# Both scan directions in one hop, full-width products behind the state hops, and a third one-hot that two engines share

## The chip, the cores and the metric

The program runs on one core of a Trainium2 chip. The metric is the device time in microseconds of one execution; lower is better. Engines by their names in the profile: PE is TensorE (its matrix products), PEld its weight loads, DVE VectorE, ACT ScalarE, POOL GpSimd, SP SyncE, which issues the transfers.

## The reference, cut to what matters

Two layers of a hybrid backbone over 640 tokens (512 latent, 128 context). In every layer one projection feeds three token mixers, and an expert stage follows. The change touches two places of a layer.

First, the RWKV-7 scan, for 4 heads of 64 and both directions d, with differential attention beside it (8 heads, softmax of two score maps):

```python
def step(S, inp):
    r_t, w_t, k_t, v_t, kk_t, a_t = inp
    sa = einsum('bhij,bhj->bhi', S, -kk_t)
    S = S * w_t[:, :, None, :] + sa[..., None] * (kk_t * a_t)[:, :, None, :] + v_t[..., None] * k_t[:, :, None, :]
    return S, einsum('bhij,bhj->bhi', S, r_t)
# run forwards for d = 0 and backwards for d = 1; the two outputs are added
```

Second, the gates of the expert layer. Per token, 128 chosen experts (a row number, a column number and a weight each) are written out as a dense 128 x 128 table of weights: the sum over the choices of (row one-hot x weight) times (column one-hot).

## The kernel before, in words

Stages run one after another, each a block in which every engine has its own instruction stream and the streams meet at semaphores. The order of work on an engine is the order of the code.

**Mixing** (`mix_stage`, once per layer). The scan works in chunks of 64 tokens, two to a tile of 128, with 5 tiles. For every step (5) and every direction (2) come 14 *hops* in a row, listed in `HOPS`. One hop is one *slot*: PE makes the hop's products in PSUM, then DVE (and in some hops ACT) copies or adds them into SBUF, and PE waits for those copies (`byv`, `bya`) before the next hop. The hops are:

- `pairs` and `lower`: products of keys with keys and receptances within a chunk (64x64 blocks), masked by DVE into `mb`, `mk`, `pwt` and `x`; `lower` also turns the keys (`bt`).
- `square1` to `square5`, `inverse`: a triangular inverse by repeated squaring. Each makes `pwt` products (L1171), `pw` products (L1175) and `x` products (L1182); DVE copies `pwt`, ACT copies `pw`, DVE adds to `x`. `inverse` also multiplies the masked keys with the values (L1188), which ACT copies into `tv`.
- `rhs`, `sa`, `state`, twice (one per chunk): the state hops, a strict chain through the state `sz`. In `state` PE makes the state's products with the receptances (L1207), the state's update (L1210, L1211) and the outputs within the chunk (L1219); DVE updates `szt` and `sz` (L1377, L1381), and in `state1` adds the outputs to `outT` (L1390).

Four heads times two chunks make 8 products of 64x64 in a group; heads and chunks lie on different halves of the partitions. A float32 product shows as two records in the trace.

Attention runs beside it in pieces. A *unit* is one head and one tile (40 units: 32 over 768 keys, the last 8 over 128). Three slots hold the pieces of a unit: behind a slot's hop, PE makes scores (L1236 to L1240) and, every second unit, value products (L1272), or turns probabilities (L1253); DVE takes row maxima (L1398), reciprocals and combines (L1412); ACT does the exponentials (L1303), scales (L1308) and copies (L1315). So the pieces are spread over about 129 of the 140 slots.

**Gates** (`gates_stage`, once per layer). Tokens come 16 at a time (an *octet*, 24 of them, two to a turn). DVE makes five tables of 128x2048 bf16: `ea` and `ob` (comparisons), and three weighted copies `oa` (L2135), since the weight is split into three bf16 parts. PE makes 48 products of them (L2152), then 4 products of the expert layer's hidden values (L1580, 128x384 float32), ACT copies the result (L2178) and, once a turn, applies the gelu (L1591). SP writes the results to DRAM and loads weights.

## Time and profile before

| what | value |
|---|---|
| median of 3 runs | 4585.85 us (4578.81 to 4588.88) |
| the profiled execution, its own time | 4598.13 us |
| its span, first to last instruction | 4596.3 us |
| mean granted clock of TensorE | 0.926 |
| mixing, first layer | 352.9 to 714.4 us |
| mixing, second layer | 2608.0 to 2973.9 us |
| gates, first and second layer | 1293.9 to 1436.7 us, 3553.4 to 3695.9 us |

The two mixing stages are 727 us of the span and the two gates stages 285 us. A stage's time is read from its own stretch; the shares over the whole span mix stages with different limits. A granted clock of 1.00 is the upper of PE's two levels (2.4 GHz), 0.50 the lower (1.2 GHz).

### The profile page before, as it was taken

The page shows a single profiled execution, that of the slowest core. Times are in us where ns is not written, and L with a number is a line of the kernel's source. Part 1 is how long each engine was busy: PE and PEld are TensorE (multiplying, and loading weights), DVE is VectorE, ACT ScalarE, POOL GpSimd, SP SyncE. Part 2 cuts the span into 40 slices and gives each one's busy share as a digit, 9 for nine tenths or more (in the row PEclk, how much of TensorE's full clock was granted, in tenths as well). Part 3 has the DMA queues.
Part 4 walks back from the last instruction along what each step waited for, and adds up shares of the span by engine and source line. Part 5 has one row for each costly group of instructions (what it writes and reads, how often), then busy time and mean ns, then how long its engine had stood idle before and what let it go on. Part 6 is the DMA issues. An engine that isn't in the chain of part 4 may idle for free. (4 is left out here: it accounts for less than half of the span.)

```text
span 4596.3 us, 73822 instructions
## 1 busy us (share of the span) xinstructions
PE 4136.2 (90%) x28014; PEld 3374.0 (73%) x28014; DVE 3534.4 (77%) x6601; ACT 1516.6 (33%) x2264; POOL 1390.6 (30%) x1046
## 2 busy tenths in 40 slices
PE   7988987899978999999989799879997989999997
PEld 5966776875556888888879477669654778888885
DVE  3456654589998999999855566437799989999996
ACT  4424532421123333333252445233111333333333
POOL 0000000006513666666400000000255055666662
PEclk8988977999989999999999789689998999999998
DMA  6230002229978999999721300031599899999994
GB/s 236 69 115 5 2 2 93 92 58 408 411 245 300 409 408 407 405 408 400 300 93 42 118 2 2 34 115 47 185 412 354 247 357 408 409 404 403 405 405 184
DMA packets 408301, 1079.58 MB, mean 235 GB/s; under 512 B 37728, under 2 KB 183392, under 8 KB 401376
## 3 DMA queue, kind: packets, MB, share of 16 engines
q1 hardware_dynamic: 260576, 539.10, 32.2%
q0 software_dynamic: 147456, 536.94, 29.4%
q8 instruction: 163, 2.67, 0.2%
q14 instruction: 106, 0.87, 0.1%
HBM read 996.47 MB, written 79.43 MB: 234 GB/s over the span
## 5 line engine op out<-in xcount | busy, mean ns | idle before, releaser
L1623 POOL DMA_INDIRECT ring<-peer_u_rows,rows x512 | 657.6, 1284 | 2221.5 <-DVEq L2020 1540.1
L1623 POOL DMA_INDIRECT ring<-peer_v,rows x512 | 708.4, 1384 | 416.1 <-DVE acc L2436 341.5
L1580 PE MATMUL ps<-h,u 128*128 128x384 f32 x2048 | 683.7, 493 | 20.8 <-PEq L1652 17.3
L204 PE MATMUL ps<-vhi,wlo 128*128 128x512 f32 x1536 | 608.4, 396 | 73.5 <-DVE wlo L2415 71.9
L2436 DVE SCALAR_TENSOR_TENSOR acc<-ring,act,acc 128x1024 f32<-128x1024 f32 x508 | 645.4, 1281 | 24.7 <-DMA ring<-peer_v,rows 18.5
L1627 DVE SCALAR_TENSOR_TENSOR ring<-ring,acc 128x1024 f32<-128x1024 f32 x512 | 621.7, 1224 | 45.6 <-DMA ring<-peer_u_rows,rows 43.2
L206 PE MATMUL ps<-vhi,whi 128*128 128x512 f32 x1536 | 604.0, 393 | 0.0
L205 PE MATMUL ps<-vlo,whi 128*128 128x512 f32 x1536 | 603.8, 393 | 0.0
L1580 PEld LDWEIGHTS ps<-h,u 128*128 128x128 f32 x2048 | 388.6, 192 | 281.1 <-issue 29.1
L204 PEld LDWEIGHTS ps<-vhi,wlo 128*128 128x128 f32 x1536 | 292.2, 190 | 148.4 <-issue 88.9
L204 PE MATMUL ps<-xhi,ulo 128*128 128x384 f32 x1024 | 345.0, 337 | 23.2 <-DVE xlo L2393 23.2
L206 PE MATMUL ps<-xhi,uhi 128*128 128x384 f32 x1024 | 344.8, 337 | 0.0
L205 PE MATMUL ps<-xlo,uhi 128*128 128x384 f32 x1024 | 344.2, 336 | 0.0
L2401 DVE TENSOR_TENSOR vlo<-v,vhi 128x1024 fp32r<-128x1024 f32 x256 | 313.2, 1223 | 31.4 <-ACT vhi L2343 30.6
L206 PEld LDWEIGHTS ps<-vhi,whi 128*128 128x128 f32 x1536 | 291.7, 190 | 61.8
L205 PEld LDWEIGHTS ps<-vlo,whi 128*128 128x128 f32 x1536 | 292.2, 190 | 59.5
L2343 ACT ACTIVATE vhi<-v 128x1024 fp32r<-128x1024 f32 x256 | 269.1, 1052 | 128.8 <-DMA v<-peer_v 128.3
L2348 ACT ACTIVATE whi<-u 128x384 fp32r<-128x384 f32 x128 | 67.1, 525 | 657.1 <-DVE u L2410 655.9
L1591 ACT ACTIVATE hh<-ps 128x384 f32<-128x384 f32 x256 | 122.9, 480 | 481.1 <-PE ps L1580 467.5
L204 PE MATMUL ps<-hhi,proj_lo 128*128 128x320 f32 x672 | 211.0, 314 | 15.2 <-DVE hlo L486 15.2
L204 PEld LDWEIGHTS ps<-xhi,ulo 128*128 128x128 f32 x1024 | 193.7, 189 | 25.9 <-DVE xlo L2393 23.5
L205 PE MATMUL ps<-hlo,proj_hi 128*128 128x320 f32 x672 | 209.3, 311 | 0.0
(356 smaller groups left out, 8077.9 us busy)
## 6 DMA issues: line engine op xcount, KB each, us to landing
u<-peer_u SPq DMA_DIRECT2D x256, 512.0 KB
v<-peer_v SPq DMA_DIRECT2D x256, 512.0 KB
gates<-stage SPq DMA_DIRECT2D x24, 2048.0 KB, 9.6
sel<-gates SPq DMA_DIRECT2D x64, 768.0 KB
mod_ring<-mod_late SPq DMA_DIRECT2D x32, 1024.0 KB, 7.7
hidden<-hh SPq DMA_DIRECT2D x128, 192.0 KB
u<-hidden SPq DMA_DIRECT2D x128, 192.0 KB
proj_raw<-w_proj SPq DMA_DIRECT2D x42, 512.0 KB, 3.7
```

Source lines behind the costliest of these rows:

```text
L204: pe.matmul(out, lhs[1], rhs[0], start=start, stop=False)
L205: pe.matmul(out, lhs[0], rhs[1], start=False, stop=False)
L206: return pe.matmul(out, lhs[0], rhs[0], start=False, stop=stop)
L1580: mm = pe.matmul(self.g.ps[:, bank, 0:ND], self.u[:, slot, kc, :], self.x[:, kc, 0:ND], start=(kc == 0), stop=(kc == KC - 1))
L1591: return self.g.nc.scalar.activation(self.hh[:, slot, :], self.g.ps[:, slot, 0:ND], ACT.Gelu)
L1623: return pool.indirect_dma_start(to, None, table, rows)
L1627: return ve.scalar_tensor_tensor(row, row, 1.0, self.acc[:, x, :], ALU.mult, ALU.mult, accum_out=self.act[x][:, slot:slot + 1])
L2343: nc.scalar.activation(v2[0][:, j, :], v[:, j % 2, :], ACT.Copy).then_inc(v_hi, 1)
L2348: nc.scalar.activation(w2[0][:, j, :], h, ACT.Copy).then_inc(w_hi, 1)
L2401: ve.tensor_tensor(v2[1][:, j, :], v[:, j % 2, :], v2[0][:, j, :].bitcast(F32), ALU.subtract).then_inc(v_lo, 1)
L2436: ve.scalar_tensor_tensor(acc, r, w, acc, ALU.mult, ALU.add).then_inc(used, 1)
```

## The change

**Mixing.** The direction is no longer a loop around the hops. A hop now does both directions: 70 slots instead of 140, each with twice the products and with DVE and ACT instructions twice as wide (128x512 where there was 128x256). Each slot is followed by two attention pieces (`PARTS_A_SLOT`). In `square2` to `square4` the power and the inverse lie side by side in one tile `px`, so that one product of 128 columns takes the place of two of 64; ACT copies `pwt` and DVE copies the power. A part of the key products is moved from `pairs` into `lower` and `square5`. In the state hops the products of the two directions alternate. `local_outputs` and its waits go away, since the outputs within a chunk are summed in PSUM ahead of the state's update. Five times a step, a product that nobody reads (`fill`, 128x256 float32) follows a state hop.

**Gates.** Of the third weighted copy DVE makes the half for 8 tokens (128x1024) and ACT the other half, in 8 small activations per octet (`weighted`). PE waits for both.

The diff, cut to its core:

```diff
-HOPS = [("pairs", "V"), ("lower", "VA"), ("square1", "VA"), ("square2", "VA"), ("square3", "VA"), ("square4", "VA"),
-        ("square5", "V"), ("inverse", "V")] + [(x + str(i), "V") for i in range(2) for x in ("rhs", "sa", "state")]
-SLOTS = [(step, dr, name, by) for step in range(TILES) for dr in range(2) for name, by in HOPS]
+HOPS = ["pairs", "lower", "square1", "square2", "square3", "square4", "square5", "inverse",
+        "rhs0", "sa0", "state0", "rhs1", "sa1", "state1"]
+XWITH = ("square2", "square3", "square4")
+SLOTS = [(step, name) for step in range(TILES) for name in HOPS]
+PARTS_A_SLOT = 2
...
+            def fill(bank):
+                pe.matmul(g.ps[:, bank, 0:CA * P], g.ident, g.proj[:, Q0, 0:CA * P], start=True, stop=True)
...
                     if n <= 5:
-                        for h in range(HA):
+                        for u in range(2 * HA):
                             for f in blocks:
-                                mm = pe.matmul(g.ps[f, B, h * CH:(h + 1) * CH], p0(f, h), pwt[f, n % 2, h, :], start=True, stop=True)
+                                mm = pe.matmul(g.ps[f, C, u * CH:(u + 1) * CH], p0(f, u), pwt[f, n % 2, u, :], start=True, stop=True)
...
+                    if name in XWITH:
+                        for u in range(2 * HA):
                             for f in blocks:
-                                mm = pe.matmul(g.ps[f, C, h * CH:(h + 1) * CH], pwt[f, n % 2, h, :], x[f, h, :], start=True, stop=True)
+                                at = u % HA * 2 * CH
+                                mm = pe.matmul(g.ps[f, (A, B)[u // HA], at:at + 2 * CH], pwt[f, n % 2, u, :], px[f, u, :, :], start=True, stop=True)
+                        mm.then_inc(xready, 1)
...
-                hop(name, dr, tile(step, dr), nx, nl)
+                hop(name, step, nx)
+                if name in ("rhs0", "rhs1", "sa0", "sa1"):
+                    fill(C)
+                elif name == "state0":
+                    fill(A)
...
+                elif name in XWITH:
+                    ve.wait_ge(xready, sums)
+                    ve.tensor_copy(pw.rearrange("p (d h) n -> p d h n", d=2), pair_sums[:, :, :, 0, :]).then_inc(byv, 1)
+                    last = ve.tensor_tensor(x.rearrange("p (d h) n -> p d h n", d=2), x.rearrange("p (d h) n -> p d h n", d=2),
+                                            pair_sums[:, :, :, 1, :], ALU.add)
...
+BY_SCALAR = 8
...
-                    for part in range(PARTS):
-                        done = ve.tensor_tensor(oa[:, o % 2, part, :, :, :], ea[:, o % 2, :, :, :], col(2 + part, o), ALU.mult)
+                    for part in range(PARTS - 1):
+                        ve.tensor_tensor(oa[:, o % 2, part, :, :, :], ea[:, o % 2, :, :, :], col(2 + part, o), ALU.mult)
+                    n = (OCT - BY_SCALAR) // DUO
+                    done = ve.tensor_tensor(oa[:, o % 2, PARTS - 1, 0:n, :, :], ea[:, o % 2, 0:n, :, :], col(1 + PARTS, o)[:, 0:n], ALU.mult)
...
+            def weighted(t, o):
+                act.wait_ge(a_eq, t * NO + (o + 1))
+                for m in range(OCT - BY_SCALAR, OCT):
+                    d, e = divmod(m, DUO)
+                    w = rest[:, PARTS - 2, bass.ds(t * GT_N + (o * OCT + m), 1)]
+                    done = nc.scalar.activation(oa[:, o % 2, PARTS - 1, d, :, e], ea[:, o % 2, d, :, e], ACT.Copy, scale=w)
+                done.then_inc(a_act, 1)
...
                 for o in range(NO):
+                    if o + 1 < NO:
+                        weighted(t, o + 1)
+                    elif not (last and q == U_RING - 1):
+                        weighted(t + 1, 0)
                     act.wait_ge(mm_ready, t * NO + (o + 3))
                     nc.scalar.activation(stage[:, b, :, o * OCT:(o + 1) * OCT], ...
```

PE in the mixing stage of the first layer, from `state0` to `state1` of one direction before (L1207 to L1219 state, L1195 `rhs`, L1202 `sa`, L1236 to L1240, L1253 and L1272 attention):

```order
L1219 MATMUL ps<-mk,vtok 64x64 x2
L1253 MATMUL ps<-keep,pd 128x128 x3
L1195 MATMUL ps<-sz,ar 64x128 x2
L1253 MATMUL ps<-keep,pd 128x128 x3
L1202 MATMUL ps<-rh,x 64x64 x4
L1236 MATMUL ps<-proj 128x384 x2
L1238 MATMUL ps<-proj 128x128 x2
L1240 MATMUL ps<-kctx,proj 128x256 x2
L1272 MATMUL ps<-pt,vtok 64x128 x8
L1272 MATMUL ps<-pt,vctx 64x128 x4
L1207 MATMUL ps<-ar,sz 128x64 x2
L1210 MATMUL ps<-sa,bt 128x128
```

The same place now, for both directions (L1171 is the unread product, L1242 `rhs`, L1249 `sa`, L1256 to L1270 state, L1286 to L1290, L1303 and L1322 attention):

```order
L1171 MATMUL ps<-proj,keep 128x256
L1303 MATMUL ps<-keep,pd 128x128 x6
L1249 MATMUL ps<-rh,px 64x64 x8
L1171 MATMUL ps<-proj,keep 128x256
L1286 MATMUL ps<-proj 128x384 x2
L1288 MATMUL ps<-proj 128x128 x2
L1290 MATMUL ps<-kctx,proj 128x256 x2
L1322 MATMUL ps<-pt,vtok 64x128 x8
L1322 MATMUL ps<-pt,vctx 64x128 x4
L1303 MATMUL ps<-keep,pd 128x128 x3
L1256 MATMUL ps<-ar,sz 128x64 x2
L1263 MATMUL ps<-mb,sa 64x64 x4
```

There are twice the products in a hop, twice the attention pieces between two hops, and an unread product ahead of the pieces.

ACT in the gates stage before, inside a turn (L2178 copies an octet's products, L1591 is the gelu):

```order
L2178 ACTIVATE stage<-ps 128x128x16
L2177 REGISTER_ALU
L2178 ACTIVATE stage<-ps 128x128x16
L1590 REGISTER_ALU
L1591 ACTIVATE hh<-ps 128x384
L2177 ISA
L2178 ACTIVATE stage<-ps 128x128x16
```

ACT there now (L2268 is that copy, L1664 the gelu, L2255 a small activation; eight of them stand ahead of each copy, the rows after the fourth are left out):

```order
L2268 ACTIVATE stage<-ps 128x128x16
L1663 REGISTER_ALU
L1664 ACTIVATE hh<-ps 128x384
L2251 REGISTER_ALU
L2255 ISA
L2255 ACTIVATE oa<-ea,rest 128x128
L2255 ISA
L2255 ACTIVATE oa<-ea,rest 128x128
L2255 ISA
L2255 ACTIVATE oa<-ea,rest 128x128
L2255 ISA
L2255 ACTIVATE oa<-ea,rest 128x128
```

ACT makes the next octet's half table before it copies this octet's products, so the copy waits behind it.

## Rows read from the trace of the kernel before

**Rows 1.** The page: busy time of each engine over the span.

```profile
PE 4136.2 (90%) x28014; PEld 3374.0 (73%) x28014; DVE 3534.4 (77%) x6601; ACT 1516.6 (33%) x2264; POOL 1390.6 (30%) x1046
```

**Rows 2.** Busy time by stretch: mixing, its steps 0 to 3, its last step, pieces.

```profile
core 0: us, PE busy (x) PEld busy (x) DVE busy (x) ACT busy (x) POOL busy (x), PEclk, DMA share, GB/s
352.90:714.40 361.50, 327.82 (x4736) 260.78 (x4736) 219.13 (x482) 152.44 (x332) 0.00 (x0) 0.84 0.01 2
352.90:650.70 297.80, 276.01 (x4000) 217.63 (x4000) 193.34 (x411) 143.08 (x302) 0.00 (x0) 0.87 0.01 2
650.70:714.40 63.70, 51.81 (x737) 43.16 (x736) 25.79 (x72) 9.35 (x30) 0.00 (x0) 0.66 0.01 2
2608.00:2973.90 365.90, 332.57 (x4736) 264.19 (x4736) 219.24 (x482) 152.51 (x332) 0.00 (x0) 0.82 0.01 2
392.60:402.80 10.20, 10.06 (x116) 7.79 (x116) 4.73 (x10) 3.94 (x8) 0.00 (x0) 0.50 0.01 2
402.80:460.90 58.10, 54.53 (x840) 42.92 (x840) 42.24 (x85) 33.14 (x66) 0.00 (x0) 1.00 0.01 2
```

**Rows 3.** DVE's groups by form, 352.9 to 650.7: count, busy us, mean ns, idle before.

```profile
L1398 DVE TENSOR_REDUCE mx<-ps 128x1 f32<-128x768 f32 x64 | 61.0, 954 | 26.7 <-PE ps L1240 26.6
...
L1381 DVE SCALAR_TENSOR_TENSOR sz<-szt,pc,keep 128x128 f32<-128x128 f32 x32 | 9.8, 349 | 0.6
...
L1377 DVE TENSOR_TENSOR szt<-sz,ps 128x256 f32<-128x256 f32 x16 | 6.7, 421 | 17.8 <-PE ps L1211 17.8
...
L1347 DVE TENSOR_TENSOR mb<-ps,mask 128x512 f32<-128x512 f32 x9 | 6.2, 692 | 10.6 <-PE ps L1151 10.6
```

**Rows 4.** PE in order of time at granted clock 1.00, squares with attention.

```profile
475.95 0.91 PE L1236 MATMUL ps<-proj 32*128 32x384 f32 x4
...
477.45 0.68 PE L1171 MATMUL ps<-pwt,pw 64*64 64x64 f32 x16
...
478.44 0.63 PE L1182 MATMUL ps<-x,pwt 64*64 64x64 f32 x16
479.00 0.55 PE L1253 MATMUL ps<-keep,pd 128*128 128x128 f32 x3
479.48 0.68 PE L1171 MATMUL ps<-pwt,pw 64*64 64x64 f32 x16
...
484.08 1.09 PE L1272 MATMUL ps<-pt,vtok 128*64 128x128 f32 x16
...
485.54 0.68 PE L1182 MATMUL ps<-x,pwt 64*64 64x64 f32 x16
```

**Rows 5.** PE in order of time at granted clock 1.00, state hops, next pairs.

```profile
491.03 0.66 PE L1207 MATMUL ps<-ar,sz 128*128 128x64 f32 x4
...
493.31 0.55 PE L1253 MATMUL ps<-keep,pd 128*128 128x128 f32 x3
493.94 0.65 PE L1195 MATMUL ps<-sz,ar 128*64 128x128 f32 x4
494.52 0.55 PE L1253 MATMUL ps<-keep,pd 128*128 128x128 f32 x3
...
502.68 1.10 PE L1151 MATMUL ps<-ar,proj 64*64 64x128 f32 x32 [1.05 <-DVE outT L1390]
```

**Rows 6.** In order of time, last step, no attention left, granted clock 1.00.

```profile
694.68 0.42 DVE L1361 COPY pwt<-ps 128x256 f32<-128x256 f32 x1 [0.76 <-PE ps L1175]
...
695.21 0.68 PE L1171 MATMUL ps<-pwt,pw 64*64 64x64 f32 x16
...
701.04 0.68 PE L1202 MATMUL ps<-rh,x 64*64 64x64 f32 x8 [0.52 <-DVE rh L1373]
```

**Rows 7.** The gates stage of the first layer: its stretch, and ACT's copies in order.

```profile
1293.90:1436.70 142.80, 133.79 (x1339) 102.09 (x1337) 136.34 (x120) 50.94 (x36) 9.59 (x6) 0.98 0.84 246
...
1320.42 1.88 ACT L2178 ACTIVATE stage<-ps 128x2048 f32<-128x2048 f32 x1 [3.51 <-PE ps L2152]
...
1325.81 1.88 ACT L2178 ACTIVATE stage<-ps 128x2048 f32<-128x2048 f32 x1 [2.26 <-PE ps L2152]
```

**Rows 8.** ACT's and PE's nearest forms: a small scaled activation; 128x384 products.

```profile
L1308 ACT ACTIVATE p<-p,sm 128x128 f32<-128x128 f32 x5 | 2.0, 401 | 11.6 <-DVE sm L1404 11.6
...
1320.22 2.80 PE L1580 MATMUL ps<-h,u 128*128 128x384 f32 x8
```

350 lines of the change are left out of this document (197 added, 153 removed).

## The prediction

> **What bounds the kernel now.** I read the page first [rows 1]: PE is busy 90% of the span and DVE 77%, but these shares mix stages. So I went by stretches [rows 2]. The first mixing stage takes 361.5 us, the second 365.9. In steps 0 to 3 (297.8 us) PE is busy 276.0 us and DVE 193.3. In the last step, when attention has run out, 63.7 us pass with PE busy 51.8 and DVE 25.8: a chain of hops with waits. The granted clock is 0.87 in steps 0 to 3 and 0.66 in the last. The reader should see that the clock is no matter of long pauses: from 392.6 to 402.8 it is 0.50 with PE busy 10.06 of 10.2 us, and in the 58 us after it is 1.00 at a busy share of 94% [rows 2].
>
> Then I read PE in order of time, for what one piece takes from its start to the next piece's start, at full clock. Two groups of 8 small products take 0.99 us (477.45 to 478.44), so 0.49 each; three turns take 0.48; the scores of a unit 1.50 (475.95 to 477.45); the values of two units 1.46 (484.08 to 485.54) [rows 4]. A `state` hop takes 2.28 us (491.03 to 493.31), `rhs` 0.58 (493.94 to 494.52) [rows 5]; `sa` has twice the records of `rhs` on a quarter of the array, I take 0.6 (its own row lasts 0.68 [rows 6]).
>
> For one step and direction: 15 groups in the squares, the inverse and its values (5 of `pwt`, 4 of `pw`, 5 of `x`, 1 with values), 7.4 us; `pairs` 1.1 [rows 5]; `lower` as one group 0.5, its four turned keys 0.6; the six state hops 2 x 3.46 = 6.9. That is 16.5 us. A unit costs 1.50 + 2 x 0.48 + 0.73 = 3.2. Steps 0 to 3 have 8 x 16.5 + 32 x 3.2 = 234 us of PE work at full clock. The stretch is 297.8 x 0.87 = 259 us of full clock. So about 25 us are waits and about 39 us are the price of the lower clock.
>
> The gates stage: DVE is busy 136.3 of 142.8 us, 120 tables of 128x2048, 24 octets of 5.68 us [rows 7]. Where PE had fallen behind at the start, the copies come 5.39 us apart (1320.42 to 1325.81): that is PE's own pace, and it is next.
>
> **The change, part by part: mixing.** All per step, both directions, full clock.
>
> Squares: the products are the same columns. 16 products of 128 columns are priced as two times 16 of 64. 0.
> Key products: they leave the four-quadrant `pairs` and come in four groups of four with 128 columns, each the columns of one group of 8. `pairs` then costs 1.1 once and the four 4 x 0.49 = 2.0, against 2 x 1.1: +0.9.
> State hops: before, 4 x 3.46 = 13.8. Now the two directions alternate between halves of the array. Turned probabilities times values do that already: 24 records take 1.46 us, 61 ns each [rows 4], while `rhs` takes 145 ns a record [rows 5]. At 61 ns `rhs` is 8 x 0.061 = 0.5 for both directions, `sa` 0.6, and `state` 2 x 0.59 for L1256 (full weights, no pairing), 16 small products 0.9, 8 update products 1.0, together 3.1. Twice 4.2 is 8.4. Five unread products of 256 columns: a product of 384 takes 2.80 / 4 = 0.70 [rows 8], so 0.47 each, 2.3. Together 10.7: -3.1.
> PE's work falls by 2.2 us a step, 9 in steps 0 to 3: 225 instead of 234. Bounds: if nothing pairs, the state hops cost 16.1 (+2.3 in place of -3.1, 22 us more in the four steps); if the unread products fall into waits throughout, 9 us less.
>
> Waits: before 25 us in four steps, 6 a step. Half as many results are waited for, but each takes longer: 0.69 us for 128x512 against 0.42 for 128x256 [rows 3]. The longest ones stand without an unread product: behind `pairs` (two of 0.69 and one of 0.42 on DVE), behind `lower` (about 2.4 us on DVE), and behind `state1` (0.69, four of 0.35, two of 0.42, 2.9 us) where before it was two of 0.35 (PE waited 1.05 [rows 5]). The two attention pieces behind each hop (2 us on average, 0.9 to 3.4) cover most of it. Queued behind these on DVE are the row maxima (0.95 each [rows 3]), and ACT's exponentials wait for those. I take 4 us a step, 16 in four; bounds 8 (all covered) and 48 (12 a step, below).
> DVE's own work falls: 11 us per direction before, 17 per step now, from the same durations. 193 becomes about 174 in four steps. It stays behind PE.
>
> Clock: 225 + 16 = 241 us at full clock. Before, 0.87. The low stretches begin around the state hops, where PE makes small products with waits between; the unread full-array products fill these. I choose half of the loss won back, 0.92: 241 / 0.92 = 262, so 36 us less. Bounds 0.87 (277) and all but the start at 1.00 (247).
>
> Last step: PE work 2 x 16.5 - 2.2 = 30.8. Waits without attention, hop by hop (DVE's time from [rows 3] and 0.2 for the two hand-overs, which [rows 6] show as 0.52 around a copy of 0.42; less an unread product where there is one): `pairs` 2.0, `lower` 2.0, `square1` 0.3, three squares of 0.9, `square5` 1.3, four `rhs`/`sa` 0.5 together, `state0` 1.6, `state1` 2.9: 13.3. Squares alone get slower: before, 1.71 a hop and direction, 3.4 for both; now 0.95 + 1.9 + 0.9 = 3.8, since the power comes only with the inverse's product. At clock 0.8 for PE's part: 30.8 / 0.8 + 13.3 = 52 against 63.7: 12 less. Bounds 44 (full clock) and 60 (0.66).
>
> Mixing together 48 us a layer. The second layer's rows repeat the first's, 96.
>
> **Gates.** DVE's five tables become four and a half: 5.68 x 0.9 = 5.1 us an octet, under PE's 5.39. PE becomes the bound: 23 x 0.29 = 6.7 us, and 0.5 at the first octet: 7 a layer. ACT now has 1.88 + 8 small activations + 0.25 of gelu. The nearest row, 128x128 scaled by a column, has 0.40 us [rows 8]: 3.2, together 5.3 at most, just under 5.39. But in turns with a gelu the copy would start late, and PE would wait up to half a microsecond per turn, 6 a layer. So between 1 and 7 a layer; since consecutive activations overlap a little, I take 7, two layers 14. DMA's share is 0.84 here [rows 7] and would be 0.88.
>
> By the Trainium skill (ScalarE: Activation LUTs, What ACT_TABLE_LOAD costs) such an activation takes 186 ns, 93 more for a pointer operand and 0.833 ns per element, and back-to-back ones overlap by about 93 ns: an estimate of 2.4 us for eight, with which the copy is not late; the single row's 0.40 agrees with the page's 0.386.
>
> **Sum.** 96 + 14 = 110 off the profiled execution's own 4598.1 us (span 4596.3 and 1.8 around it): 4488. The median of the runs is 12 below that execution, so I predict 4475.
>
> **Rivals.**
> *The unread products buy no clock* (0.22). For: the lower clock comes while PE is 99% busy [rows 2], so full queues are no guard. Then steps 0 to 3 take 277 (-21), the last 60 (-4), a layer -25, with gates -64: 4522.
> The Trainium skill (TensorE: Matmul & The Clock Gate, Why this matters for your kernels) ties the fall of the clock to idle gaps of PE. By that rule short waits cost no clock and the fillers are wasted work; the rows at 392.6 disagree, so I hold the granted clock of the rows above it, and the rule's result for this change is that of this rival.
> *The clock stays full* (0.25). Against: `pairs` and `lower` keep their waits. Steps 0 to 3 take 247 (-51), the last 44 (-19), 140 and 14 together: 4432.
> *DVE and PE take turns* (0.12). Row maxima of two pieces sit ahead of the next hop's copy, and the short hops `rhs` and `sa` hide none of it: a wait of 12 a step, 225 + 48 = 273, at 0.9 clock 303: steps 0 to 3 lose 5, the last gains 12, a layer 7, with the gates 28: 4558. With waits of 8 a step they take 257 / 0.9 = 286, a layer gives 24, and the time is 4524. For: DVE idled 26.7 us for scores before row maxima [rows 3].
> *Slower* (0.07). One mechanism: the three uncovered waits of 2 to 3 us a step pull the clock down. The rest gives 4 + 7 = 11 a layer, so it decides when steps 0 to 3 pass 309 us, at a clock of 241 / 309 = 0.78 against 0.87 now.
> *My forecast* (0.34), its own range 4445 to 4505.
>
> **Numbers.** A measurement of this kernel tells 0.2%, 9 us, from no change. Faster: all but the slower case and half of the weak end of the turn-taking, 0.89; same 0.04; slower 0.07. The range runs from a bit under the full clock with all waits covered (4400) to a bit over the no-clock case with some turn-taking (4545).
>
> **What would show it.** Mixing stretches of about 313 us with clock near 0.9 and PE still over 90% busy in steps 0 to 3; `rhs` for both directions as long as for one now; a last step near 52 us. In the gates, copies 5.39 us apart and PE idle less than 0.1 us an octet. It would be wrong if PE waited on DVE for more than 5 us a step, if the granted clock were below 0.87, or if the copies in the gates waited for the small activations.

## The result, and the profile after

The changed kernel takes 4503.56 us (median of 4 runs, 4498.04 to 4510.91) against 4584.15 us for the kernel before (4 runs, 4578.81 to 4588.88), a ratio of 0.982 with a 95% interval of 0.9801 to 0.9838. That is 80.6 us faster; 110 were forecast. The time lies inside the range, 28.6 us above the point. The profiled execution itself took 4500.27 us, 97.9 less than that of before.

The shares of busy time over the span say nothing here: PE is at 90% as before [rows 1], while ACT has 109 us more work (1625.5 us against 1516.6) without being what the time waits for. The stretches do say something (same columns as [rows 2]; in this order: first mixing, its steps 0 to 3, its last step, second mixing, its steps 0 to 3, the gates of the first layer up to the end of their last copy):

```profile
352.80:685.70 332.90, 283.68 (x4306) 223.06 (x4306) 189.69 (x391) 151.23 (x312) 0.00 (x0) 0.91 0.01 2
352.80:636.50 283.70, 246.34 (x3624) 192.41 (x3624) 168.72 (x335) 141.21 (x283) 0.00 (x0) 0.92 0.01 2
636.50:685.70 49.20, 37.35 (x683) 30.65 (x683) 20.97 (x57) 10.02 (x29) 0.00 (x0) 0.90 0.01 2
2567.00:2890.70 323.70, 274.69 (x4306) 215.60 (x4306) 189.51 (x391) 151.45 (x312) 0.00 (x0) 0.94 0.01 2
2567.00:2841.50 274.50, 237.33 (x3624) 184.94 (x3624) 168.54 (x335) 141.44 (x283) 0.00 (x0) 0.95 0.01 2
1261.00:1394.80 133.80, 128.98 (x1339) 100.76 (x1337) 124.80 (x120) 106.89 (x228) 9.06 (x6) 0.99 0.89 263
```

The first mixing stage goes from 361.5 to 332.9 us, the second from 365.9 to 323.7 [rows 2]: 70.8 us together. What the reader should see is the split. In steps 0 to 3 of the first layer PE is idle for 283.70 - 246.34 = 37.4 us, where before it was 297.80 - 276.01 = 21.8. So PE waits more than before, and yet the stretch is 14 us shorter, since PE's busy time fell from 276.0 to 246.3 us: there is less to do, and above all the granted clock is 0.92 and not 0.87. In the last step the clock is 0.90 and not 0.66. Two stretches of one program with the same code, steps 0 to 3 of the two layers, differ by 9.2 us, at clocks of 0.92 and 0.95.

Where PE waits is told by its costliest group in the same stretch (busy us, mean ns, idle before it and who ended that). First the turned probabilities before the change, then after:

```profile
L1253 PE MATMUL ps<-keep,pd 128*128 128x128 f32 x196 | 38.3, 304 | 3.1 <-issue 2.2 <-ACT pt L1315 0.8
```

```profile
L1303 PE MATMUL ps<-keep,pd 128*128 128x128 f32 x195 | 35.6, 291 | 25.1 <-issue 11.4 <-DVE outT L1493 9.2 <-DVE pd L1487 3.8
```

25 of the 37 us of idle time stand before one kind of attention piece. 3.8 of them are waits for VectorE to make the probabilities (`pd`). PE in order of time shows both forms of it (start, duration, idle before):

```profile
458.44 0.61 PE L1322 MATMUL ps<-pt,vctx 128*64 128x128 f32 x8
459.53 0.52 PE L1303 MATMUL ps<-keep,pd 128*128 128x128 f32 x3 [0.49 <-DVE outT L1493]
...
479.02 0.49 PE L1303 MATMUL ps<-keep,pd 128*128 128x128 f32 x3
480.45 0.52 PE L1303 MATMUL ps<-keep,pd 128*128 128x128 f32 x3 [0.94 <-issue]
480.81 0.56 PE L1256 MATMUL ps<-ar,sz 128*128 128x64 f32 x4
```

Two pieces now stand behind one hop, and turns and values go to the same PSUM bank. At 458 the value products are followed by a turn, which waits for VectorE to copy their result out. At 479 two turns follow each other, and the second waits for ScalarE's copy of the first. The row names no releaser, but the program has PE wait there for that copy, and in the trace the copy runs from 479.87 to 480.35 and the turn starts at 480.45. It is 1.79 us from 479.02 to the next hop where two turns had cost 0.96 of PE's time. Before, each piece stood behind a hop of its own, whose products covered the copy.

The state hops of a step where the clock is 1.00 (to compare with [rows 5], where the same names stand for one direction):

```profile
488.35 0.66 PE L1242 MATMUL ps<-sz,ar 128*64 128x128 f32 x8
488.94 0.70 PE L1171 MATMUL ps<-proj,keep 128*128 128x256 f32 x2
489.47 0.49 PE L1303 MATMUL ps<-keep,pd 128*128 128x128 f32 x3
...
491.39 0.68 PE L1249 MATMUL ps<-rh,px 64*64 64x64 f32 x16
492.00 0.70 PE L1171 MATMUL ps<-proj,keep 128*128 128x256 f32 x2
...
494.33 0.56 PE L1256 MATMUL ps<-ar,sz 128*128 128x64 f32 x4
...
496.19 0.49 PE L1268 MATMUL ps<-sa,bt 64*128 64x128 f32 x4
...
497.28 0.91 PE L1286 MATMUL ps<-proj 32*128 32x384 f32 x4
```

These times run from the start of one group to the start of the next. `rhs` for both directions takes 0.59 us (488.35 to 488.94), where one direction took 0.58; `sa` takes 0.61, the whole `state` hop 2.95 (494.33 to 497.28), an unread product 0.53 (488.94 to 489.47).

The last step, without attention in the way:

```profile
636.50 1.10 PE L1181 MATMUL ps<-ar,proj 64*64 64x128 f32 x32 [2.45 <-DVE outT L1466]
...
651.08 1.15 PE L1203 MATMUL ps<-pwt,px 64*64 64x64 f32 x32
...
652.06 1.91 PE L1219 MATMUL ps<-px,pwt 64*64 64x128 f32 x32
...
653.91 0.33 PE L1303 MATMUL ps<-keep,pd 128*128 128x128 f32 x1
...
654.84 1.15 PE L1203 MATMUL ps<-pwt,px 64*64 64x64 f32 x32 [0.60 <-DVE px L1436]
```

`pairs` waits 2.45 us for the end of `state1`. A square hop takes 3.76 us (651.08 to 654.84) and ends in a wait for the copy of the power.

In the gates, ACT in order of time (small activations L2255, the copy L2268) and the copies of both layers by line (duration min/median/max, first and last start):

```profile
1285.60 1.88 ACT L2268 ACTIVATE stage<-ps 128x2048 f32<-128x2048 f32 x1 [0.16 <-PE ps L2229]
...
1288.78 2.49 ACT L2255 ACTIVATE oa<-ea,rest 128x128 bf16<-128x128 bf16 x8
1291.14 1.85 ACT L2268 ACTIVATE stage<-ps 128x2048 f32<-128x2048 f32 x1
1293.23 2.49 ACT L2255 ACTIVATE oa<-ea,rest 128x128 bf16<-128x128 bf16 x8 [0.24 <-DVE ea L2205]
1296.37 1.88 ACT L2268 ACTIVATE stage<-ps 128x2048 f32<-128x2048 f32 x1 [0.65 <-PE ps L2229]
```

```profile
L2268 ACT ACTIVATE stage<-ps x48: 1848/1877/1880, 1269.9 to 3598.3; 128x2048 f32<-128x2048 f32 x48
L2255 ACT ACTIVATE oa<-ea,rest x384: 419/428/447, 1262.3 to 3593.1; 128x128 bf16<-128x128 bf16 x192
```

The gates stretch of the first layer takes 133.8 us where it took 142.8 [rows 7], that of the second 135.2 (3465.0 to 3600.2) where it took 142.8 (3552.8 to 3695.6): 17 us for both. Two copies span 10.77 us, 5.39 each. From the first to the last copy of a layer it is 123.1 and 123.7 us where it was 130.5 and 132.2: 16 us for both. Eight small activations take 2.49 us together. Half of the copies (24 of 48) wait for PE, the others start as soon as the activations ahead of them are done, still only 5.2 to 5.5 us behind the copy before.

### The profile page after: what moved, and what is told of

It is laid out like the page before. It is cut to its first block and busy times, and to the rows that moved or that the text cites. A ratio compares the mean times of both kernels' runs of the same rounds, so it can differ in the third digit from the quotient of the medians.

```text
span 4498.5 us, 72458 instructions
## 1 busy us (share of the span) xinstructions
PE 4027.4 (90%) x27154; PEld 3289.6 (73%) x27154; DVE 3453.4 (77%) x6419; ACT 1625.5 (36%) x2608; POOL 1396.0 (31%) x1046
## 5 line engine op out<-in xcount | busy, mean ns | idle before, releaser
L1664 ACT ACTIVATE hh<-ps 128x384 f32<-128x384 f32 x256 | 123.1, 481 | 465.2 <-PE ps L1653 465.1
L206 PE MATMUL ps<-hhi,proj_hi 128*128 128x320 f32 x672 | 209.4, 312 | 0.0
```

Source lines behind the costliest of these rows:

```text
L206: return pe.matmul(out, lhs[0], rhs[0], start=False, stop=stop)
L1664: return self.g.nc.scalar.activation(self.hh[:, slot, :], self.g.ps[:, slot, 0:ND], ACT.Gelu)
```

## The experiments

Two readings were to be told apart. One says that the extra waits of PE cost time, and that whoever takes them away is paid for it. The other says that the time is set by the granted clock, which the unread products raise, and that less idle time is given back as a lower clock. Letters for theories in the expectations are labels of that expectation alone. Each ratio is to the kernel before, run on the same chip. The time given first is the median; the profile is of one execution, which can lie up to 17 us beside it (the table at the end of this section says how far).

### The parts of the change by themselves

**gates_only**: the mixing as before, the gates as changed. (The edit is the second half of the diff above.)

> The kernel before with the gates part of the change alone; mixing is as before. If the two parts are independent: gates stages about 135 us instead of 143, copies 5.39 us apart, PE never waiting for ScalarE; time 4584 - 15 = 4569, ratio 0.9965. If the small activations made the copies late somewhere, under 4 us a layer, ratio 0.998 or more. The mixing stretches stay at 361 and 366 us.

4576.58 us (10 runs), ratio 0.9971 (0.9960 to 0.9982): 13 us. The copies of a layer span 123.1 and 123.8 us, as in the changed kernel. The mixing stages, whose code is that of before, take 367.6 and 361.7 us, where before they took 361.5 and 365.9: the same code differs by 4 to 6 us from one execution to another.

**mix_only**: the gates as before, the mixing as changed.

```diff
-                    for part in range(PARTS - 1):
-                        ve.tensor_tensor(oa[:, o % 2, part, :, :, :], ea[:, o % 2, :, :, :], col(2 + part, o), ALU.mult)
-                    n = (OCT - BY_SCALAR) // DUO
-                    done = ve.tensor_tensor(oa[:, o % 2, PARTS - 1, 0:n, :, :], ea[:, o % 2, 0:n, :, :], col(1 + PARTS, o)[:, 0:n], ALU.mult)
+                    for part in range(PARTS):
+                        done = ve.tensor_tensor(oa[:, o % 2, part, :, :, :], ea[:, o % 2, :, :, :], col(2 + part, o), ALU.mult)
...
-                    pe.wait_ge(a_act, t * NO + (o + 1))
```

> The changed kernel with the gates as they were before: VectorE makes all one-hots of the third level again; the mixing is all of the change. If the two parts add, this is the changed kernel's 4503.6 us and what the gates' part gave by itself, 0.29% of the time (13 us): 4516 to 4518. If the mixing's part gave less than that because its gain is limited by what the clock takes, the sum need not hold: 4525 or more would say that the gates give more beside the new mixing than alone.

4530.56 us (5 runs), ratio 0.9873 (0.9853 to 0.9892). By the letter this is the case in which the gates give more beside the new mixing than alone: 27 us instead of 13. The profile says that it isn't the gates. Their copies span 132.2 us in each layer, 9.1 and 8.5 more than in the changed kernel. The rest stands in the mixing, whose code is the same as in the changed kernel:

```profile
352.60:695.20 342.60, 296.20 (x4306) 231.43 (x4306) 189.86 (x391) 151.07 (x312) 0.00 (x0) 0.87 0.01 2
2581.90:2917.50 335.60, 287.99 (x4306) 225.10 (x4306) 189.75 (x391) 151.63 (x312) 0.00 (x0) 0.90 0.01 2
```

342.6 and 335.6 us at clocks 0.87 and 0.90, where the changed kernel has 332.9 and 323.7 at 0.91 and 0.94. As many records, DVE busy for the same time, and 22 us of difference that go with the clock. The two profiled executions lie further apart (37.7 us) than the medians (27.0 us), so some 11 of these 22 us are only the choice of the execution. The two ratios of the parts multiply to 0.9844, 0.0024 from the whole's 0.982, about as much as the intervals leave open.

**no_fill**: the changed kernel without the unread products.

```diff
                 hop(name, step, nx)
-                if name in ("rhs0", "rhs1", "sa0", "sa1"):
-                    fill(C)
-                elif name == "state0":
-                    fill(A)
```

> The changed kernel without its five unread products a step. Theory A, the unread products keep the clock up: the granted clock of steps 0 to 3 falls from 0.92 to 0.95 back to about 0.87 and that of the last step from 0.90 to about 0.7; PE's work falls by 12 us a layer, the clock takes back about 20 in steps 0 to 3 and 8 in the last step; in all about 16 us a layer slower, 4503 + 30 = 4535. Theory B, the gain of clock comes from the denser hops alone: the clock stays above 0.9 and the kernel gets up to 10 us a layer faster, 4485 to 4500.

4549.38 us (6 runs), ratio 0.9922 (0.9903 to 0.9941). The unread products are worth 46 us in the changed kernel, where the forecast of the theory that they keep the clock up was 30; the merged hops without them, next to the gates alone, give 4576.6 - 4549.4 = 27 us. The first mixing and its last step:

```profile
354.10:702.60 348.50, 294.72 (x4256) 233.14 (x4256) 189.80 (x391) 150.79 (x312) 0.00 (x0) 0.83 0.01 2
650.10:702.60 52.50, 38.11 (x673) 32.17 (x673) 21.01 (x57) 10.02 (x29) 0.00 (x0) 0.79 0.01 2
```

The whole stage's clock is 0.83, about what the kernel before had (0.84), but the last step's is 0.79 and not 0.66. This profiled execution was the fastest of the six, 17 us below their median.

**before_fill**: the kernel before with the unread products, behind the same hops of each direction (50 a layer, where the change has 25).

```diff
                 hop(name, dr, tile(step, dr), nx, nl)
+                if name in ("rhs0", "rhs1", "sa0", "sa1"):
+                    pe.matmul(g.ps[:, C, 0:CA * P], g.ident, g.proj[:, Q0, 0:CA * P], start=True, stop=True)
+                elif name == "state0":
+                    pe.matmul(g.ps[:, A, 0:CA * P], g.ident, g.proj[:, Q0, 0:CA * P], start=True, stop=True)
```

> The kernel before with five unread 128x256 products behind the state hops of each direction, ten a step, nothing else. Theory F, the clock is all that the change won in steps 0 to 3 and the unread products bring it: the granted clock of a mixing stage rises from 0.84 to 0.92 or more, the products cost up to 23 us a layer, and with the clock's 30 to 40 us back the time is 4560 to 4585 (ratio 0.994 to 1.000), the last step near 55 us. Theory M, the merged hops are needed for it: the clock stays below 0.88 and the time rises by 15 us or more a layer, 4610 or more.

4561.35 us (4 runs), ratio 0.9939 (0.9921 to 0.9957). More work and nothing else, and 28 us faster:

```profile
353.40:703.40 350.00, 324.06 (x4836) 255.55 (x4836) 219.52 (x482) 152.47 (x332) 0.00 (x0) 0.93 0.01 2
643.80:703.40 59.60, 50.20 (x789) 40.94 (x789) 26.40 (x75) 10.13 (x33) 0.00 (x0) 0.83 0.01 2
```

The stage's clock goes from 0.84 to 0.93, in the second layer from 0.82 to 0.94, with 100 records more. This settles the rival that the unread products buy no clock.

**fill_double**: each unread product twice.

```diff
             def fill(bank):
-                pe.matmul(g.ps[:, bank, 0:CA * P], g.ident, g.proj[:, Q0, 0:CA * P], start=True, stop=True)
+                for _ in range(2):
+                    pe.matmul(g.ps[:, bank, 0:CA * P], g.ident, g.proj[:, Q0, 0:CA * P], start=True, stop=True)
```

> The changed kernel with each unread product made twice. PE's work rises by 12 us a layer at full clock. Theory C1, the clock is already won: stages get 6 to 12 us longer, 4515 to 4525. Theory C2, there is more clock to win: granted clock of the first layer's steps 0 to 3 from 0.92 to 0.97 and more, which returns 15 us, and the time is 4495 to 4505.

4512.45 us (5 runs), ratio 0.9839 (0.9816 to 0.9861): beside the changed kernel no difference that can be told, if any a loss. The mixing stages take 334.8 and 336.6 us at clocks of 0.93 and 0.92, where the changed kernel has 0.91 and 0.94: the second product of each pair adds work and buys no more clock.

**no_alternate**: in `rhs`, `sa` and the state's update, first all products of one direction, then those of the other. (The small products of `state` keep their order.)

```diff
-                        for c in range(CA):
-                            for dr in range(2):
+                        for dr in range(2):
+                            for c in range(CA):
                                 mm = pe.matmul(g.ps[hs[dr], A, c * P:(c + 1) * P], ar[:, dr, c, ts[dr], 0, hs[dr]], sz[:, dr, c, :], start=True, stop=True)
...
-                        for c in range(CA):
-                            cols = slice(c * P, (c + 1) * P)
-                            for dr in range(2):
+                        for dr in range(2):
+                            for c in range(CA):
+                                cols = slice(c * P, (c + 1) * P)
```

> The changed kernel with the products of rhs, sa and the state's update in the order of before, one direction after the other, so that neighbours lie on the same half of the array. Theory Q, the alternation makes neighbours run side by side: rhs takes 1.1 us instead of 0.6, sa 1.1 instead of 0.6, the update 1.9 instead of 1.1, together 3.6 us a step and 18 us a layer at full clock, 4503 + 36 = 4539 (less if a fuller PE raises the clock). If the order does not matter, the same durations and 4503.

4538.53 us (6 runs, 4516.76 to 4551.96), ratio 0.9877 (0.9854 to 0.9899), 35 us slower than the changed kernel by the medians, 26 by the ratios. At clock 1.00:

```profile
478.44 0.67 PE L1242 MATMUL ps<-sz,ar 128*64 128x128 f32 x8
479.03 0.70 PE L1171 MATMUL ps<-proj,keep 128*128 128x256 f32 x2
...
481.49 0.96 PE L1249 MATMUL ps<-rh,px 64*64 64x64 f32 x16
482.38 0.70 PE L1171 MATMUL ps<-proj,keep 128*128 128x256 f32 x2
...
486.29 0.48 PE L1268 MATMUL ps<-sa,bt 64*128 64x128 f32 x2
...
487.92 0.70 PE L1171 MATMUL ps<-proj,keep 128*128 128x256 f32 x2
```

`rhs` takes 0.59 us in either order: not the alternation halves it per direction, but that both stand in one group. `sa` goes from 0.61 to 0.89, the update from 1.09 (496.19 to 497.28) to 1.63. That is 2 x (0.28 + 0.54) = 1.6 us a step, 8 a layer, 16 in all. The other 10 to 19 us go with the clock: the two mixing stages of the profiled execution have 0.88 and 0.86 instead of 0.91 and 0.94. The Trainium skill (TensorE: Matmul & The Clock Gate, Why this matters for your kernels) says that products of few rows run at the same time if they lie on different row groups; the update and `sa` agree. It says the same of products of few output columns that lie on different column groups; `rhs` is of that kind (all 128 rows, its outputs on either half), and there no gain shows, 0.59 in either order.

### Taking the new waits away

**turns_apart**: one turn of every second unit is moved, so that no two turns stand in one slot.

```diff
-    parts = ([("scores", u, 0), ("values", u - 3, 0)],
-             [("turn", u - 2, 0)],
+    parts = ([("scores", u, 0), ("values", u - 3, 0)] + [("turn", u - 2, 0)] * (u % 2),
+             [("turn", u - 2, 0)] * (1 - u % 2),
              [("turn", u - 2, 1)])[part]
```

> The changed kernel with one of two turns that stand directly behind each other moved one slot earlier, behind the scores of that slot. Theory P, two pieces in one slot that write the same PSUM bank make PE wait for the copy of the first: 16 pairs of turns a layer at 0.65 to 0.8 us, PE's idle time before the turns falls from 25 us in steps 0 to 3 to about 14, a layer gets 8 to 12 us shorter, 4503 - 20 = 4483. Theory D, PE waits for VectorE, whose wide copies and row maxima take turns with the hops: the idle time only moves to the next hop, under 3 us a layer, 4498 to 4508.

4505.66 us (5 runs), ratio 0.9818 (0.9799 to 0.9838): the same time, and in the range of theory D. Of the 25.1 us before turns 18.1 are left. The waits named "issue", 11.4 us, are gone, those for the outputs remain (9.7), and those for VectorE's `pd` rise from 3.8 to 8.3: in part the idle time moved, as D says. But not all of it did. Steps 0 to 3 of the first layer are 11 us shorter than in the changed kernel, at a higher clock:

```profile
354.00:626.60 272.60, 239.40 (x3624) 186.84 (x3624) 169.90 (x338) 141.89 (x284) 0.00 (x0) 0.94 0.01 2
```

It is the last step, whose hops are those of the changed kernel, that takes the time back: 59.6 us at a clock of 0.72 where the changed kernel has 49.2 at 0.90, and 56.6 at 0.77 in the second layer.

**all_apart**: besides, the values come ahead of the scores, and VectorE copies the outputs first, so that no turn stands right behind values either.

```diff
+    parts = ([("values", u - 3, 0), ("scores", u, 0)] + [("turn", u - 2, 0)] * (u % 2),
+             [("turn", u - 2, 0)] * (1 - u % 2),
...
+                    for what, v, k in attention_parts(virtual):
+                        if what == "values":
+                            out(v)
                     if part <= 1 and u < len(UNITS):
                         row_max(u, part)
```

> As turns_apart, and the value products stand ahead of the scores with VectorE copying their result before the row maxima, so that the turn behind them finds the bank free. Theory P: another 16 waits a layer of 0.5 to 1.4 us go, PE's idle time before the turns falls to under 5 us in steps 0 to 3, a layer gets 18 to 24 us shorter than the changed kernel, 4503 - 42 = 4461, and its steps 0 to 3 come near the 241 us at full clock of the forecast. Theory D: under 5 us a layer, 4495 or more.

4511.28 us (5 runs), ratio 0.9825 (0.9804 to 0.9846). The turns of the first layer, the stage and its steps 0 to 3:

```profile
L1303 PE MATMUL ps<-keep,pd 128*128 128x128 f32 x196 | 38.7, 308 | 11.6 <-DVE pd L1487 7.2 <-issue 3.8 <-DVE outT L1493 0.4
```

```profile
355.00:695.10 340.10, 297.65 (x4306) 233.20 (x4306) 190.25 (x391) 148.94 (x312) 0.00 (x0) 0.87 0.01 2
355.00:640.80 285.80, 256.56 (x3624) 198.98 (x3624) 169.72 (x338) 139.01 (x283) 0.00 (x0) 0.88 0.01 2
```

The idle time before turns falls from 25.1 to 11.6 us and that for outputs from 9.2 to 0.4. So the waits for the outputs were where I had put them. But theory P had under 5 us left before turns and a time of 4461 us, and it is 11.6 us and 4511, in D's range: the waits for `pd` went from 3.8 to 7.2. Steps 0 to 3 take 285.8 us, not less than 283.7, at a clock of 0.88 and not 0.92. That this edit lowered the clock is not shown, since mix_only, with the unaltered order, has 294.6 us at 0.86 and, in the second layer, 287.5 at 0.90. Beside the latter all_apart's second layer, 281.5 us at the same 0.90, is 6 us shorter. This profiled execution is also the slowest of the five.

**fill_between**: the unread product stands between the two attention pieces and not ahead of both.

```diff
                 for part in range(PARTS_A_SLOT * slot, PARTS_A_SLOT * (slot + 1)):
+                    if part % PARTS_A_SLOT:
+                        if name in ("rhs0", "rhs1", "sa0", "sa1"):
+                            fill(C)
+                        elif name == "state0":
+                            fill(A)
```

> The changed kernel with the unread product of a slot moved from behind the hop to between the slot's two attention pieces, where PE waits for a copy. Theory P (PE waits between the two pieces of a slot, 0.5 to 0.8 us each time): the unread product costs nothing there, steps 0 to 3 get 1.5 to 2.5 us shorter each at the same clock, 4503 - 16 = 4487. Theory C (the granted clock decides, and it does not care for work that merely fills these pauses): within 5 us of the changed kernel, or above it if the clock falls.

4498.69 us (5 runs), ratio 0.9809 (0.9791 to 0.9826). Some of the idle time before turns is filled (19.3 us left of 25.1). Its first mixing takes 329.6 us at 0.90, its second 325.6 at 0.92; against the changed kernel that is within what can't be told apart.

**power_first, power_between, power_apart**: the square hop's power is made ahead of `x`, so that VectorE copies it while PE multiplies `x`. The second adds the edit of fill_between, the third also that of all_apart.

```diff
                         mm.then_inc(ready, 1)
...
                     if name in XWITH:
                         for u in range(2 * HA):
                             for f in blocks:
-                                at = u % HA * 2 * CH
-                                mm = pe.matmul(g.ps[f, (A, B)[u // HA], at:at + 2 * CH], pwt[f, n % 2, u, :], px[f, u, :, :], start=True, stop=True)
+                                mm = pe.matmul(g.ps[f, B, u * CH:(u + 1) * CH], pwt[f, n % 2, u, :], px[f, u, 1, :], start=True, stop=True)
...
                 elif name in XWITH:
+                    ve.tensor_copy(pw, by_unit(A)).then_inc(byv, 1)
                     ve.wait_ge(xready, sums)
```

> The changed kernel with the order inside the square hops turned: the power's products (64 wide, in a PSUM bank of their own) come ahead of the two independent products and the x products, so VectorE copies the power while TensorE multiplies x. Theory W (what is left in the last step is a chain of copies that TensorE waits for, and time comes back wherever a copy is taken off that chain): a square hop of the last step goes from 3.76 to about 2.9 us, the last step of a layer from 49.2 to 46.5 us, steps 0 to 3 hardly change because TensorE has attention to do there; time 4495 to 4500 us. Theory P (the granted clock gives back whatever idle time is taken away): the hop falls to 2.9 at full clock, but the mean clock of the last step falls below 0.89 and the time stays within 0.1% of the changed kernel, 4500 to 4508.

> The edit of power_first together with that of fill_between (the products whose results nobody reads stand between the rows of the state hops instead of at their end; 4498.7 by itself). Theory W: both gains add, 4498.7 less 6 us, about 4490 to 4493. Theory P: no better than fill_between, 4497 to 4501.

> The edit of power_between together with all_apart's order of the attention pieces (no two turns to one PSUM bank in the same slot; 4511.3 by itself, with less idle time of TensorE and a lower clock). Theory W: 4485 or less, since idle time is taken away in all steps. Theory P: at or above 4500, with a mean clock of a layer's mixing lower than in power_between, as all_apart showed.

4510.11 us (4490.94 to 4527.95), ratio 0.9824 (0.9797 to 0.9851); 4503.57 us, ratio 0.9812 (0.9798 to 0.9825); 4499.07 us, ratio 0.9803 (0.9788 to 0.9819), 5 runs each. The hop of power_first in order of time, and its last step:

```profile
662.72 1.15 PE L1203 MATMUL ps<-pwt,px 64*64 64x64 f32 x32
663.70 1.10 PE L1209 MATMUL ps<-px,pwt 64*64 64x64 f32 x32
664.64 1.10 PE L1218 MATMUL ps<-px,pwt 64*64 64x64 f32 x32
665.60 1.15 PE L1203 MATMUL ps<-pwt,px 64*64 64x64 f32 x32
```

```profile
636.50:687.40 50.90, 41.42 (x779) 34.51 (x779) 21.25 (x57) 10.08 (x29) 0.00 (x0) 0.80 0.01 2
```

The hop takes 2.88 us (662.72 to 665.60) where it took 3.76, as both theories had it, and the wait for the copy is gone. The last step takes 50.9 us where it took 49.2: its clock is 0.80 and not 0.90. In power_between, with the same hop, it takes 47.0 and 47.1 us at 0.88, where fill_between, the kernel without this edit, has 50.5 and 52.6 at 0.86 and 0.82; there the step is 3.5 and 5.5 us shorter, about what theory W asked of power_first (46.5 us). Two products of 64 columns also turn out to cost as much as one of 128 (0.94 and 0.96 against 1.85 from 652.06 to 653.91), so merging them had brought nothing by itself. All three kernels are at or above the changed kernel's time or less than 0.2% below it. None of the three came out where a theory had it. power_first (4510) lies above both ranges, power_between (4503.6) above its 4497 to 4501, and power_apart, at 4499, just under the bound of 4500 for theory P and 14 us above what W asked for, with a granted clock of 0.940 to 0.942 over the whole program, no lower than power_between's (0.939 to 0.943). So the theory that waits pay their full length (W) is refuted for the time of the kernel, and its rival, that the clock gives the idle time back, is not shown: the last step's clock of 0.80 lies within what kernels with the old square hops have (0.72 to 0.93).

### All mixing stages side by side

Duration and granted clock of both layers, and their product, which is the stage's length in microseconds of full clock. The clock has two digits, so a product is good to about 2 us. The last column is the profiled execution less the median of that kernel's runs.

| kernel | first layer | product | second layer | product | profiled less median |
|---|---|---|---|---|---|
| before | 361.5, 0.84 | 304 | 365.9, 0.82 | 300 | +14 |
| gates_only | 367.6, 0.82 | 301 | 361.7, 0.84 | 304 | 0 |
| before_fill | 350.0, 0.93 | 326 | 347.2, 0.94 | 326 | +1 |
| no_fill | 348.5, 0.83 | 289 | 345.5, 0.84 | 290 | -17 |
| no_alternate | 347.5, 0.88 | 306 | 355.7, 0.86 | 306 | +13 |
| mix_only | 342.6, 0.87 | 298 | 335.6, 0.90 | 302 | +7 |
| all_apart | 340.1, 0.87 | 296 | 331.6, 0.90 | 298 | +9 |
| turns_apart | 332.2, 0.90 | 299 | 328.5, 0.92 | 302 | -4 |
| changed kernel | 332.9, 0.91 | 303 | 323.7, 0.94 | 304 | -3 |
| power_first | 332.7, 0.91 | 303 | 332.7, 0.91 | 303 | 0 |
| power_apart | 332.7, 0.89 | 296 | 321.2, 0.93 | 299 | 0 |
| power_between | 320.5, 0.94 | 301 | 331.4, 0.90 | 298 | -4 |
| fill_between | 329.6, 0.90 | 297 | 325.6, 0.92 | 300 | 0 |
| fill_double | 334.8, 0.93 | 311 | 336.6, 0.92 | 310 | 0 |

The product column is the point of this table. Before it is 304 and 300, in the changed kernel 303 and 304: most of what the change gained in the mixing is clock. Its parts work in opposite ways: merging the directions takes 12 us a layer off (no_fill), the unread products add 14 back, and in exchange the clock goes from 0.83 to about 0.92. In before_fill they add 24 and buy 0.10 of clock. Inside the product, PE's busy time times the clock fell, from 275 and 273 to 258 and 258, while PE's idle time rose from 33.7 and 33.3 us to 49.2 and 49.0: what the merged hops save in work, the new waits take.

The product has one weakness. Waits of PE for other engines don't get shorter when PE's clock rises, so they weigh more at a high clock: the same mixing code has 298 and 302 in mix_only, at clocks of 0.87 and 0.90, and 303 and 304 at 0.91 and 0.94. At the clock of before, the changed code would therefore stand a little below 304 and 300; I estimate from these four numbers that some 5 us a layer of the 28.6 and 42.2 gained are not clock.

How far two executions of one code can part is seen where mix_only and the changed kernel come to the same place (each time the stretch ahead of a fall of the clock, then the low stretch; first the changed kernel):

```profile
538.80:542.80 4.00, 2.47 (x25) 1.52 (x22) 2.44 (x6) 3.12 (x7) 0.00 (x0) 1.00 0.00 0
542.90:553.00 10.10, 9.62 (x62) 6.79 (x62) 3.75 (x7) 3.85 (x8) 0.00 (x0) 0.50 0.00 0
```

```profile
531.50:535.50 4.00, 2.47 (x24) 1.54 (x20) 2.45 (x5) 3.12 (x7) 0.00 (x0) 1.00 0.00 0
535.60:593.50 57.90, 54.28 (x414) 39.25 (x412) 24.22 (x49) 18.27 (x34) 0.00 (x0) 0.50 0.00 1
```

In both, PE is busy for 2.47 of 4 us, and the clock falls. In the changed kernel it is back after 10 us, in mix_only after 58, with PE busy for 94% of them. This one stretch is most of why mix_only's steps 0 to 3 have 0.86 and the changed kernel's 0.92.

## Why the prediction was right, and where its sizes were off

**The forecast's kind of case was right.** It had the clock won back in part, neither at no gain (0.87, ruled out by before_fill) nor at full clock. The granted clock of steps 0 to 3 is 0.92 and 0.95, where 0.92 was chosen. Of the signs named ahead, `rhs` and the last step came out, and PE's share in steps 0 to 3 did not: 87% and 86%, not over 90%, and the mixing stretches are 332.9 and 323.7 us, not about 313.

**The mis-sized term is the waits in steps 0 to 3** ("I take 4 us a step, 16 in four"). PE is idle for 37.4 us at 0.92, 34 us of full clock, where 16 were forecast; before it was 21.8 at 0.87, 19. What PE's work costs held: 283.7 x 0.92 less 34 is 227 us, forecast 225. I had taken "the two attention pieces behind each hop" as cover for VectorE's copies and had not asked whether the pieces wait for each other. They share one PSUM bank, and 25 us of the idle time stand there, some 21 of them for this reason (11.4 and 9.2 us; the other 3.8 are for `pd`). Had I read in the old trace that turns and values of one bank were never neighbours, this would have been a line of the sum. It is also the one step in which the case "DVE and PE take turns" was partly true: the waits lie between its 8 and 12 us a step, but most of it was waited for at the turns and not for the copies of the hops.

**What this wait costs in time is open in part.** By the sum, 18 us too many a layer should have cost 18 / 0.92 = 20 us; the first layer's steps 0 to 3 came out 283.7 instead of 262, 22 more, the second's 274.5, 12 more at a clock of 0.95. So the mis-sized term is of the size of the miss in the mixing, 25 us for both layers. But none of the kernels that take some of this wait away (turns_apart, all_apart, power_apart) is faster than the changed one beyond the noise. Two things are mixed here. At equal clock these kernels are somewhat shorter: in the second layer's steps 0 to 3 turns_apart has 271.9 us and power_apart 271.7 at 0.95, beside 274.5, and all_apart 281.5 at 0.90, beside mix_only's 287.5 (the clock's two digits leave up to 3 us of this open). And the clock differs by more than that between executions of the same mixing code. That the clock falls because idle time is taken away is not shown.

**A reading of the clock that was too short.** The prediction took the row from 392.6 to 402.8 (clock 0.50 with PE busy 10.06 of 10.2 us) as a sign that the clock is no matter of pauses. The row ahead of it says otherwise:

```profile
389.00:392.60 3.60, 1.76 (x37) 1.17 (x35) 3.10 (x6) 1.86 (x4) 0.00 (x0) 1.00 0.00 0
```

Ahead of the fall PE was busy for less than half of the time, with pauses of 1.05 us before `pairs` and 0.93 us before `lower`. The choice of 0.92 rested on the unread products filling such places, which fits; that it was the middle between two bounds, and came out at 0.92 and 0.95, is in part luck.

**Work of the hops.** `rhs` 0.59 (0.5 forecast), `sa` 0.61 (0.6), `state` 2.95 (3.1), an unread product 0.53 (0.47), all within 0.15 us. The reason for `rhs` was wrong: no_alternate has it at 0.59 too. For the update the alternation works as argued, 1.09 against 1.63.

**Last step.** Forecast 52 with waits of 13.3; measured 49.2 with PE idle 49.20 - 37.35 = 11.9. A square hop 3.76 (3.8), the wait at `pairs` 2.45 (2.9). The clock of 0.90 is above the 0.8 taken, and the waits were 1.4 us less. Before, 63.7 x 0.66 is 42 us of full clock, and now 49.2 x 0.90 is 44: this step's net gain too is all clock, with work saved and unread products added in between. no_fill has 52.5 us at 0.79 in both layers, so 11 of the 14.5 us come with the merged hops and the rest with the unread products. How much is chance is not known: this step's clock is 0.90 in the changed kernel, 0.93 in mix_only with the same code and 0.72 in turns_apart.

**Gates.** The forecast was 7 a layer with PE as the next bound at 5.39 us; the copies are 5.39 apart and span 7.4 and 8.5 us less. ScalarE's eight activations take 2.49 us together and not 3.2: one lasts 0.428, but they overlap. The estimate from the Trainium skill (ScalarE: Activation LUTs, What ACT_TABLE_LOAD costs) was 2.4, and the trace agrees with it better than with my sum of single rows. So the copy is on time, and PE sets the pace. The stretches from the first table to the end of the last copy gain 9.0 and 7.6 us. By itself this part gives 13 us (gates_only, 14 forecast).

**The sum.** Mixing gave 71 us where 96 were forecast, gates 17 where it was 14, and 10 us came in other stages, for which I had nothing. Nine of these stand between the end of the mixing and the gates (579.5 to 575.3 us, and 578.9 to 574.3). They can't be put down to the change: up to the first copy of the gates it is 589.9 us before and 584.2 now, but 582.9 in gates_only and 582.4 in mix_only, each with half of the change. Their cause is open, and that they helped the forecast is luck; with no gain there it would have been 39 us off. That makes 98 of 110 from one profiled execution to the other. The execution before had been 12 us above the median known then, that of after is 3 below its own: these 15.6 us and the 12 that the sum had too many are the 28 us between 4475 and 4503.6. The base for a prediction is good to a quarter of a per cent at best.

## What to carry to other kernels

Multiply a stretch's length by its granted clock before and after: that product says better than the length whether work was saved, and here most of the mixing's gain was clock. Mind that waits for other engines weigh more in it at a high clock. A few full-array products that nobody reads, put where small products follow each other, can be worth more than they cost, and twice as many are not better. When two pieces of side work are put behind one hop, look whether they share a buffer; and when removing a proven wait brings nothing, read the clock of every stretch, and of a second kernel with the same code there, before blaming the edit for it.

## What the runs showed of the hardware that was not expected

- Ahead of each of the eight falls of the clock in the changed kernel's mixing stages (from 8 us behind their start on), PE was busy for between 45% and 72% of 4 us, where its share of the stage is 85%. Not every such stretch is followed by a fall, and busy time is not all that counts: in the kernel before the clock also fell behind 3.70 busy us of 4.00 (569.5 to 573.5). The Trainium skill (TensorE: Matmul & The Clock Gate, Why this matters for your kernels) ties a lower clock to idle gaps of PE between bursts of products; the rows agree in that falls follow pauses, but no single long gap is needed: ahead of the fall at 542.8 the longest is 1.53 us. What in the sequence of PE's work decides is open.
- A lower clock itself makes PE's idle time smaller, since PE's own products then last longer and cover more of the waits (a record of L1286 lasts 583 ns on average in the one, 603 in the other of the two stretches named next). With the same mixing code steps 0 to 3 of the first layer have 37.4 us of idle time at 0.92 in the changed kernel and 34.5 us (294.60 - 260.11) at 0.86 in mix_only. So all_apart's 29.2 us (285.80 - 256.56) at 0.88 are not all due to its edit, and such pairs don't say which is cause and which effect.
- The same code gets another clock from one layer to the next and beside another change elsewhere: 0.91 and 0.94 in the two layers of the changed kernel, 0.87 and 0.90 in mix_only, 22 us in sum. Differences of about 0.5% between single profiled executions can be the clock alone.
- Sixteen products of 128 columns on a quarter of the array (1.85 us for 32 records) cost as much as twice sixteen of 64 (0.94 and 0.96).
- Eight activations of 128x128 of 0.428 us each take 2.49 us in a row, 0.31 each.
